# Keys of a second attention layer: transposed by VectorE in 32x32 blocks in place of TensorE and a copy

## The reference

```python
def shared_kv(x, positions, gain, w_kv):
    b, s = x.shape[:2]
    kv = (rms_norm(x, gain) @ w_kv).reshape(b, s, DIFF_HEADS, 2 * DIFF_HEAD_DIM + DIFF_V_DIM)
    k1 = rope(kv[..., :DIFF_HEAD_DIM], positions)
    k2 = rope(kv[..., DIFF_HEAD_DIM:2 * DIFF_HEAD_DIM], positions)
    v = kv[..., 2 * DIFF_HEAD_DIM:]
    return k1, k2, v
...
        s1 = jnp.einsum('bqhd,bkhd->bhqk', q1_blk, k1).astype(jnp.float32) * scale
        s2 = jnp.einsum('bqhd,bkhd->bhqk', q2_blk, k2).astype(jnp.float32) * scale
```

## Time and profile before

| | us |
|---|---|
| median of 3 runs (lowest to highest) | 2191.18 (2191.09 to 2191.27) |
| span of the profiled execution | 2189.5 |
| PE busy | 2179.9 |
| PEld busy | 1888.0 |
| DVE busy | 1428.4 |
| ACT busy | 1227.5 |

### The profile page before, as it was taken

One profiled execution on the slowest core, in us unless ns is written; L12 is line 12 of the kernel. 1 busy time (PEld: TensorE's weight loads), 2 busy tenths in 40 slices (PEclk: granted clock), 3 DMA queues, 4 the chain that ended last, 5 costly groups with the idle time before them and its releaser, 6 DMA issues.

```text
span 2189.5 us, 33021 instructions
## 1 busy us (share of the span) xinstructions
PE 2179.9 (100%) x11793; PEld 1888.0 (86%) x11793; DVE 1428.4 (65%) x1941; ACT 1227.5 (56%) x1714; POOL 5.4 (0%) x18
## 2 busy tenths in 40 slices
PE   9999999999999999999999999999999999999998
PEld 8989988888888888888888888888888888888887
DVE  5757756777777767444476577567777776774444
ACT  5746645665666665444365557466566656554443
POOL 0000000000000000000000000000000000000000
PEclk9999999999999999999999999999999999999999
DMA  8565265556566666666666543656656566566664
GB/s 286 176 186 174 87 202 175 184 179 201 179 187 190 191 186 202 207 190 197 190 183 191 187 151 126 195 153 191 201 180 187 189 192 186 182 222 196 192 193 152
DMA packets 203041, 406.12 MB, mean 185 GB/s; under 512 B 12925, under 2 KB 16375, under 8 KB 202191
## 3 DMA queue, kind: packets, MB, share of 16 engines
q1 hardware_dynamic: 202223, 400.29, 58.6%
q0 software_dynamic: 736, 4.72, 0.6%
HBM read 402.86 MB, written 2.10 MB: 185 GB/s over the span
## 4 chain that ended last, share of the span: by engine, by line
PE 99%; DMA 0%; DVE 0%; ACT 0%; SPq 0%; DVEq 0%; issue 0%
PE ps L574 43%; PE ps L620 29%; PE ps L628 15%; PE ps L658 3%; PE ps L668 3%; PE ps L1183 1%; PE ps L734 1%; PE ps L872 0%; PE ps L901 0%; PE ps L797 0%; PE ps L878 0%; PE ps L762 0%; PE ps L805 0%; PE ps L834 0%; DMA w_raw<-in_a_w_mem_kv 0%; PE ps L792 0%
## 5 line engine op out<-in xcount | busy, mean ns | idle before, releaser
L1998 DVE TENSOR_TENSOR w_lo<-w_raw,w_hi 128x1024 fp32r<-128x1024 f32 x608 | 736.8, 1223 | 477.3 <-ACT w_hi L1386 473.0
L1386 ACT ACTIVATE w_hi<-w_raw 128x1024 fp32r<-128x1024 f32 (+1 forms) x624 | 645.1, 1046 | 459.9 <-PE ps L574 320.6
L620 PE MATMUL ps<-xT,w_hi 128*128 128x512 f32 x2816 | 673.6, 391 | 0.0
L620 PEld LDWEIGHTS ps<-xT,w_hi 128*128 128x128 f32 x2816 | 517.0, 188 | 100.6 <-issue 0.6
L628 PEld LDWEIGHTS ps<-xT,w_lo 128*128 128x128 f32 x2816 | 361.6, 191 | 14.3 <-DVE w_lo L1998 0.4
L628 PE MATMUL ps<-xT,w_lo 128*128 128x256 f32 x2816 | 367.4, 283 | 0.0
L574 PE MATMUL ps<-w_hi,hT_hi 128*128 128x512 f32 x704 | 273.9, 389 | 0.0
L574 PE MATMUL ps<-w_hi,hT_lo 128*128 128x512 f32 x704 | 273.9, 389 | 0.0
L574 PE MATMUL ps<-w_lo,hT_hi 128*128 128x512 f32 x704 | 273.9, 389 | 0.0
L574 PE MATMUL ps<-w_hi,xT 128*128 128x512 f32 x640 | 203.1, 392 | 0.0
L574 PEld LDWEIGHTS ps<-w_lo,hT_hi 128*128 128x128 f32 x704 | 132.2, 188 | 27.5
(11 more groups left out here) (296 smaller groups left out, 2144.2 us busy)
## 6 DMA issues: line engine op xcount, KB each, us to landing
w_raw<-in_ffn_w_in SPq DMA_DIRECT2D x352, 512.0 KB, 4.1
w_raw<-in_ffn_w_out SPq DMA_DIRECT2D x176, 512.0 KB, 4.6
w_raw<-in_shared_w_kv SPq DMA_DIRECT2D x48, 512.0 KB, 4.0
w_raw<-in_a_w_o SPq DMA_DIRECT2D x32, 512.0 KB, 4.6
w_raw<-in_b_w_in SPq DMA_DIRECT2D x32, 512.0 KB, 4.5
w_raw<-in_b_w_o SPq DMA_DIRECT2D x32, 512.0 KB, 4.7
w_raw<-in_a_w_mem_kv SPq DMA_DIRECT2D x16, 512.0 KB, 6.4
w_raw<-in_b_w_mem_kv SPq DMA_DIRECT2D x16, 512.0 KB, 4.3
```

What stands on the lines that cost most here:

```text
L620: mm = nc.tensor.matmul(ps[:, base + m4, :].rearrange("p (a n) -> p a n", a=2), w_hi[:, slot, cols], xT[:, :, 2 * k + c, :], start=k == c ...
L1386: nc.scalar.activation(w_hi[:, s % R, 0:width], w_raw[:, s % R, 0:width], ACT.Copy)\
L1998: nc.vector.tensor_tensor(w_lo[:, s % R, :], w_raw[:, s % R, :], w_hi[:, s % R, :].bitcast(F32), ALU.subtract)\
```

## The change

PE's transposes of the keys and ACT's copies to `kT_b` are taken out. In their place DVE, behind the six instructions of the rotation, does 16 transposes (`turn_keys`): each reads 32 partitions (32 tokens of each token half) x 128 elements and writes 32 partitions of `kT_b` x 128 elements, as four blocks of 32x32. ACT's copy of the next tile into `scratch` waits until DVE has done that (`rope_ready`), and PE waits for the last of them once, ahead of `BQ` tile 2.

```diff
@@ GROUPS
-          ("N", 8), ("C", 1), ("N", 12), ("C", 6), ("C", 6), ("N", 6), ("N", 8), ("C", 1)]
+          ("N", 8), ("C", 1), ("N", 12), ("C", 0), ("C", 6), ("N", 6), ("N", 8), ("C", 1)]
@@ TensorE
             for j in range(1, BH):
                 skv_tile(j)
-                if j >= 3:
-                    pe.wait_ge(tr_copied, c0 + j - 2)
-                rope_transpose(4 + (j - 1) % 2, kb_blocks, 7 + j)
...
             bq_tile(0, n_parts())
-            pe.wait_ge(tr_copied, c0 + 4)
-            rope_transpose(5, kb_blocks, 13)
             bq_tile(1, n_parts())
...
+            pe.wait_ge(rope_ready, 13)
             bq_tile(2, n_parts(), after=beside_bq2)
@@ ScalarE
                 if j:
-                    copy_transposed(kT_b[:, 2 * j - 2:2 * j, :].rearrange("p h s -> p (h s)"),
-                                    4 + (j - 1) % 2)
+                    act.wait_ge(rope_ready, 7 + j)
                 raw_epilogue(SKV_T + j, 256, SKV + (j + 1) * DSTEPS)
...
-            copy_transposed(kT_b[:, 10:12, :].rearrange("p h s -> p (h s)"), 5)
+            act.wait_ge(rope_ready, 13)
             raw_epilogue(BQ_T, 512, BQ + DSTEPS)
@@ VectorE
+            def turn_keys(j):
+                rows = raw[:, :].rearrange("p (t n) -> p t n", t=TT)
+                for i in range(4):
+                    for o in range(4):
+                        src = rows[32 * i:32 * (i + 1), :, 0:2 * P]\
+                            .rearrange("p t (g d) -> p t g d", g=2)[:, :, :, 32 * o:32 * (o + 1)]
+                        dst = kT_b[32 * o:32 * (o + 1), 2 * j:2 * j + 2, :]\
+                            .rearrange("p g (t n) -> p t g n", t=TT)[:, :, :, 32 * i:32 * (i + 1)]
+                        d = nc.vector.transpose(dst, src)
+                return d
...
+                if keys is not None:
+                    link(d)
+                    d = turn_keys(keys)
                 d.then_inc(rope_ready, 1)
...
-                rotate(pair_act, SKV_T + j + 1, 512, 256, 32, HD // 2)
+                rotate(pair_act, SKV_T + j + 1, 512, 256, 32, HD // 2, keys=j)
```

More of the change, by code:

```diff
@@ L1228, in skv_first_tile @@
                         x_group(k + 2, range(TT))
-            kb_blocks = [rot[:, 512 * t + P * g:512 * t + P * (g + 1)]
-                         for g in range(2) for t in range(TT)]
             skv_tile = lambda j, **kw: product(SKV + j * DSTEPS, DSTEPS, SKV_T + j, xbT_hi, xbT_lo,
                                                n_parts(), **kw)
-            c0 = groups_before(T_KB, "C")
             skv_first_tile()
@@ L2156, in _, with rotate @@
             tmp = scratch[:, 1].rearrange("p a b -> p (a b)")
-            def rotate(semaphore, value, row, width, c0, half, twice=False, src=None):
+            def turn_keys(j):
[8 more added lines that the diff above has]
+                return d
+            def rotate(semaphore, value, row, width, c0, half, twice=False, src=None, keys=None):
                 dve.wait_ge(semaphore, value)
```

## The result

The change makes the kernel slower: 2211.22 us (median of 5 runs, 2210.00 to 2211.49) against 2191.27 (5 runs, 2191.09 to 2192.36). The ratio is 1.0088, 95% interval 1.0078 to 1.0099. The span of the profiled execution is 2208.2 us, where it was 2189.5: 18.7 more. The profiled execution is the shortest of the five (2210.00, mean granted clock 0.997); the three at 2211.22 to 2211.49 have 0.996.

The account below looks back on a forecast made before the run. PE was taken to bound the kernel, busy 2179.9 of 2189.5 us. Stalls of 15.5 us less 2.8 gained made it 12.7 us slower, 2204; the forecast's own span was 2199 to 2210 (71%), the range 2197 to 2218.

Parts of the forecast that it names:

- What leaves PE: Tile ends in the shared-keys stage: each group of four PE transposes costs 0.47 us, six groups 2.8 us gained.
- What leaves ACT: Tile end: without transposes and copy to `kT_b`, ACT's raw copy starts 0.87 us earlier, a head start for DVE only.
- The price of a transpose: DVE behind the rotation: 0.284 + 0.02, rounded up to 0.31 us each; 16 are 4.96 us.
- The pair on changing partitions: First-layer DVE instructions that swap partition halves: no overlap, 422 ns each, starts 0.44 us apart; taken as the price rule.
- the instructions on the same partitions: Rival: DVE transposes overlap like such instructions, 0.20 to 0.21 us each; 2.6 us slower, 2193.8; 12%.
- The deadline: Room for DVE's block before PE needs the next split: 2.54 us in tiles 1 to 5, 1.54 in tile 0.
- The delay stayed single: Behind the late step: DVE's splits take 1.35 us against PE's 2.72, load four us in hand, so no further stall.
- The load theory: From the experiments: DVE's 29 us of added work slows the stage wherever it stands; 2195 to 2210 us for moved blocks.
- The sum: Whole kernel: PE stalls of 15.5 us lost, 2.8 gained, 12.7 us slower.
- The clock: Rival: stalls lower PE's clock, matmuls take twice as long, six falls add 6 x 2.7; 2220; 5%.
- The late starts: PE's stalls at the late split: 2.42 us for each of tiles 1 to 5, 3.42 for tile 0, together 15.5.
- a dearer transpose: Rival: DVE transposes cost up to 0.45 us each; 26 us slower, 2217; 10%.

Follow-up runs that it names:

- The wide transpose: The change with one transpose of 128 x 512 elements per tile instead of 16, crossing between partition groups left out: 2188.23 us, ratio 0.9984.
- the moved block in pieces: The change with its 16 transposes in four pieces of four, ahead of the splits of steps 6 to 9 of PLAN: 2188.12 us, ratio 0.9983.
- own partitions: The change with each transpose writing the same 32 partitions that it reads, so scores are of other numbers: 2197.36 us, ratio 1.0027.
- the turned order: The change with its 16 transposes reordered: written partitions stay for four in a row, those read change at each: 2211.79 us, one run.
- the block moved by four steps: The change with all 16 transposes in one block ahead of the splits of step 7 of the next tile: 2188.91 us, ratio 0.9990.
- the filled stalls: The change with small bf16 matmuls into an unused PSUM bank ahead of PE's six waits for the late split: 2205.76 us, ratio 1.0068.

## Why the prediction was right, point by point

- **What leaves PE**, 2.8 us: right. The wide transpose and the moved block in pieces gained 2.8 and 2.9.
- **What leaves ACT**: right. Its raw copy starts 0.10 us behind the tile's last matmul (1148.23 + 0.39 to 1148.72), and DVE's rotation ends at 1152.60, 4.14 us after PE has begun the next tile; forecast 4.13. The timeline of PE in the changed kernel, the tile's last matmul and the next tile's first:

```profile
1148.23 0.39 PE L574 MATMUL ps<-w_hi,xbT_lo 128*128 128x512 f32 x1
1148.46 0.39 PE L574 MATMUL ps<-w_hi,xbT_hi 128*128 128x512 f32 x1
```

The timeline of ACT in the same kernel:

```profile
1148.72 0.84 ACT L1518 ACTIVATE scratch<-ps,rstd 128x256 f32<-128x256 f32 x2 [0.99 <-PE ps L574]
```

- **The price of a transpose**: 0.31 was forecast; 0.316 from start to start was measured (5.05 less 0.30, by 15), with a duration of 303 ns. The pair on changing partitions was the right row, and the instructions on the same partitions (0.20) would have given 2194. The runs with own partitions and with the turned order show that it is the move that costs, by what is read or by what is written. The Trainium skill's 311 ns for a bf16 transpose of 128x128 ("VectorE: DVE Perf Modes", The three transpose paths) is 3% above the 303 ns of these, which are float32 and 32x128.
- **The deadline**: right in place, and 0.14 us short in size. The late split is that of step 5 in tile 1 and of step 3 behind it. The forecast's 3.42 and 2.42 are how much later the step's first matmul starts. By the starts that is 3.55 (1136.39 to 1140.17, less 0.23) and 2.56 (1156.39 to 1159.18, less 0.23). From the first transpose to the next split it is 5.07 us (1152.64 to 1157.71), where the forecast had 4.96; the other 0.03 is spread over the chain. The waits in the profile, 3.39 and 2.40, are 0.16 shorter than the late starts, because they count from the end of the last matmul (0.39 long), whose successor would have started 0.23 behind its start. That they agree with 3.42 and 2.42 to 0.03 is luck: two differences cancel. The delay stayed single in each tile, and the block moved by four steps stalls almost nothing. The load theory is excluded by that. Tile 4, where the clock stayed up, is 24.46 us long, forecast 24.2.
- **The sum**, 12.7 us: too small by 6 to 7 (18.7 in the span, 20.0 in the medians), from three terms.
  - *The clock*, 4.7 us in the profiled execution: the step that failed. It was given as a rival with 5% and left out of the forecast's sum, and a fall in the stage was named as a sign that the prediction is wrong. It came true behind three of six stalls. Behind the second one the nine intervals between matmul starts from 1159.18 to 1162.85 take 3.67 us in place of 2.04; 0.11 of that is the next term, 1.5 the clock. The other two cost 1.6 each. That this is the clock and not something else is shown by the filled stalls: from the first matmul of tile 1 to the first of `BQ` tile 1 they take 147.75 us, the change 152.47. The forecast's size for the rival, six falls of 2.7 us, was too large. The median of the runs lost 1.3 us more than the profiled span did. The kernel with the turned order, which has the same waits and four falls in its trace, took 2211.79, so a fourth fall would account for it; no trace of such a run of the change was taken.
  - *Starting again*, 0.7: the first interval behind a stall is 0.34 in place of 0.23 where the clock stays up, 0.11 for each of six. I had put nothing into the sum for it.
  - *The late starts*, 0.9: 16.4 in place of 15.5, as above.
  - Late starts 16.4, 0.7 to start again and 4.7 of the clock, less 2.8, are 19.0. The stage shows 19.1. In the kernel before it takes 133.33 us, from 1123.26 to this matmul, the first of `BQ` tile 1 (timeline of PE):

```profile
1256.59 0.48 PE L574 MATMUL ps<-w_hi,xbT_hi 128*128 128x512 f32 x1
```

In the changed kernel it takes 152.47 us, from the first matmul of tile 1 to the first of `BQ` tile 1 (timeline of PE):

```profile
1123.02 0.39 PE L574 MATMUL ps<-w_hi,xbT_hi 128*128 128x512 f32 x1
...
1275.49 0.39 PE L574 MATMUL ps<-w_hi,xbT_hi 128*128 128x512 f32 x1
```

The measured 2211 lies above the forecast's own 2199 to 2210, and inside the range by luck: the range was kept wide for a dearer transpose, which did not occur, and left out the clock, which did. With the clock kept up by the fills, 2205.8, the time is within the forecast's own 2199 to 2210. So the account of the block and its deadline holds, and the clock is what it lacked.

## What to carry to other kernels

An engine's average slack (here 8 us of 22) says nothing about a block of work put at one place in its order; compare the block with the room ahead of the very next instruction that the bounding engine waits for, and put it, or split it, where the queue ahead is full. The same change cost 20 us with the 96 transposes behind the rotation and gave 2.9 with them behind the later splits, where DVE is busy for 95% of the tile. If a stall of TensorE can't be avoided, price it with the lower clock behind it, or give it something to do.

## What the hardware showed beyond the forecast

- The granted clock fell behind stalls of 1.9 and 2.1 us (one each, in two kernels), behind three of six of 2.4 to 3.4 us in the change (in the kernel with the turned order behind four of six), and behind all six of 4.95 to 5.93 us. Behind the 17 stalls of 0.4 to 1.1 us it never fell. Six of these 17 are the filled ones, where PE had worked until then. At 1.2 GHz the matmuls of 128x512 started 0.43 us apart, and this lasted for 6 to 13 of them. The Trainium skill ("TensorE: Matmul & The Clock Gate", Why this matters for your kernels) warns of idle gaps between bursts of matmuls, and these runs agree: the clock fell behind gaps, and behind nothing else in this stage. Why one stall of 2.40 us brings it and the next of the same length doesn't is open.
- A float32 transpose on DVE of 32 partitions x 128 elements: 303 ns on changing partitions, 0.32 us from start to start; 271 ns (mean) where most stay on the same, 0.20 us from start to start there. A change of what is read or of what is written is enough.
- A wait of PE in the profile is shorter than what PE loses by it: here by 0.16 us, and the first interval behind it is 0.11 us longer.
